# Two-block network on one Trainium2 core: the mixer's v projection as seven products of half matrices per 1024 columns, instead of eight

## The reference, cut to what matters

```python
def gmlp_mixer(h, w_in, ln_g, ln_b, w_s, b_s, w_out):
    u, v, z = jnp.split(h @ w_in, 3, axis=-1)      # h: 512 x 1024, w_in: 1024 x 6144
    u = jax.nn.gelu(u)
    v = layer_norm(jax.nn.gelu(v), ln_g, ln_b)     # v: 512 x 2048
    ...                                            # s: v mixed over tokens by w_s, plus b_s
    y = u * s * jax.nn.silu(z)
    return y @ w_out
```

## Time and profile before

| | us |
|---|---|
| median of 3 runs | 947.67 (946.54 to 948.96) |
| profiled execution, whole time | 946.47 |
| its span (first to last instruction) | 944.7 |
| PE busy | 899.6 (95%) |
| POOL busy | 637.6 (67%) |
| DVE busy | 445.0 (47%) |
| ACT busy | 282.3 (30%) |
| mean granted TensorE clock | 0.988 |
| bytes moved | 84.31 MB, mean 89 GB/s |

### The profile page before, as it was taken

How to read it: one execution, slowest core, us unless ns; L and a number is a source line. 1 busy time by engine, 2 the same in 40 slices (tenths; PEclk the granted TensorE clock), 3 DMA queues, 4 the chain that set the end, 5 groups by cost and what they waited for, 6 DMA issues and landing times.

```text
span 944.7 us, 11929 instructions
## 1 busy us (share of the span) xinstructions
PE 899.6 (95%) x4304; PEld 747.8 (79%) x4304; DVE 445.0 (47%) x782; ACT 282.3 (30%) x711; POOL 637.6 (67%) x702
## 2 busy tenths in 40 slices
PE   4999899899999989999999999999997999988997
PEld 3788788788887768888888888888876988877886
DVE  4125446755226252000844400444468868778634
ACT  4124333331225232114111111111113435765632
POOL 7677474547789667776977766777787598546343
PEclk9999999999999999999999999999999999999999
DMA  7433222233422223332222232222231222112202
GB/s 208 133 112 98 81 67 67 68 108 116 134 89 68 90 89 112 91 110 91 89 91 90 89 110 89 89 90 90 89 106 50 68 91 87 48 46 67 67 2 89
DMA packets 71866, 84.31 MB, mean 89 GB/s; under 512 B 11264, under 2 KB 53760, under 8 KB 71808
## 3 DMA queue, kind: packets, MB, share of 16 engines
q1 hardware_dynamic: 71808, 83.54, 28.1%
HBM read 81.44 MB, written 2.10 MB: 88 GB/s over the span
## 4 chain that ended last, share of the span: by engine, by line
PE 79%; DVE 8%; POOL 5%; ACT 3%; issue 2%; DMA 1%; SPq 0%; POOLq 0%; DVEq 0%; ACTq 0%
PE bank L1469 24%; PE bank L1470 24%; PE bank L1471 24%; POOL wlo L591 2%; PE bank L1636 2%; POOL ms L543 1%; POOL rstd L546 1%; ACT junk L654 1%; PE bank L1609 1%; POOL whi L584 1%; DMA resid<-in_x 1%; PE bank L1664 1%; DVE smB L1367 1%; DVE pT L1421 1%; DVE raw L1318 1%
## 5 line engine op out<-in xcount | busy, mean ns | idle before, releaser
L591 POOL TENSOR_TENSOR wlo<-raw,whi 128x512 fp32r<-128x512 f32 x280 | 383.3, 1390 | 0.0
L584 POOL TENSOR_SCALAR whi<-raw 128x512 fp32r<-128x512 f32 x280 | 184.3, 676 | 265.2 <-PE bank L1471 257.0
L1469 PE MATMUL bank<-actB_hi,whi 128*128 128x512 f32 (+1 forms) x416 | 160.0, 385 | 0.8 <-POOL wlo L591 0.8
L1470 PE MATMUL bank<-actB_lo,whi 128*128 128x512 f32 (+1 forms) x416 | 159.3, 383 | 0.0
L1471 PE MATMUL bank<-actB_hi,wlo 128*128 128x512 f32 (+1 forms) x416 | 159.2, 383 | 0.0
L1469 PE MATMUL bank<-whi,actA_hi 128*128 128x512 f32 x304 | 122.6, 403 | 7.2 <-DVE actA_lo L983 4.5
L1471 PE MATMUL bank<-whi,actA_lo 128*128 128x512 f32 x304 | 120.6, 397 | 0.0
L1470 PE MATMUL bank<-wlo,actA_hi 128*128 128x512 f32 x304 | 120.4, 396 | 0.0
L1469 PEld LDWEIGHTS bank<-actB_hi,whi 128*128 128x128 f32 x416 | 78.7, 189 | 15.5 <-DVE big L1281 0.9
L1471 PEld LDWEIGHTS bank<-actB_hi,wlo 128*128 128x128 f32 x416 | 78.6, 189 | 15.4
L1470 PEld LDWEIGHTS bank<-actB_lo,whi 128*128 128x128 f32 x416 | 78.6, 189 | 14.2
(11 more groups left out here) (205 smaller groups left out, 1340.3 us busy)
## 6 DMA issues: line engine op xcount, KB each, us to landing
raw<-in_a_w_in SPq DMA_DIRECT2D x48, 512.0 KB, 3.7
raw<-in_w_in SPq DMA_DIRECT2D x32, 512.0 KB, 3.7
raw<-in_a_w_out SPq DMA_DIRECT2D x16, 512.0 KB, 3.3
raw<-in_b_w_in SPq DMA_DIRECT2D x16, 512.0 KB, 3.4
raw<-in_w_out SPq DMA_DIRECT2D x8, 512.0 KB, 3.9
raw<-in_w_ple_gate SPq DMA_DIRECT2D x8, 512.0 KB, 3.3
raw<-in_b_w_out SPq DMA_DIRECT2D x8, 512.0 KB, 3.4
resid<-in_x SPq DMA_DIRECT2D x4, 512.0 KB, 7.9
```

Source lines behind the costliest of these rows:

```text
L584: pool.tensor_scalar(H, src[:, i * HALF:(i + 1) * HALF], 1.0, 1.0, ALU.mult, ALU.mult).then_inc(w_hi, 1)
L591: ins = pool.tensor_tensor(L, src[:, i * HALF:(i + 1) * HALF], H.bitcast(f32), ALU.subtract)
L1469: M(out_, whi_, xhi_, start=start, stop=False)
L1470: M(out_, whi_, xlo_, start=False, stop=False)
```

## The change

**The computation.** The 512 tokens by 1024 rows of h are cut into quarters: A11 is tokens 0 to 255 by the lower 512 of k, A12 the same tokens by the upper 512, A21 and A22 the other 256 tokens. A group of 1024 columns of the weights is cut into B11, B12, B21, B22 in the same way. Instead of eight products of quarters there are seven (numbered m), for each of the two groups g:

| m | activations | weights |
|---|---|---|
| 0 | A11 | B11 |
| 1 | A12 | B21 |
| 2 | A21 - A22 | B11 + B12 |
| 3 | A11 - A21 | B12 + B22 |
| 4 | A21 - A22 - A11 | B11 + B12 + B22 |
| 5 | A12 + A21 - A22 - A11 | B22 |
| 6 | A22 | B11 + B12 + B22 + B21 |

A product q = 7 g + m is two blocks `("S", "v4", q, r)` of 12 products on PE, one for each 128 of its 256 tokens. 14 products make 28 blocks, 336 products of 512 columns where there were 384. A unit now serves 24 of them, and there are 14.

**Sums of weights.** They are made in the places of the raw weights by accumulating transfers: the quarters come in the order of `LOADS7` into three places A, B (the four rows of `raw`) and G (rows 1 and 2 of `gain`), each as two halves of 512 KB; loads 3, 4, 6 and 7 of a group are issued by POOL with `accum_op=ALU.add`, on top of what lies there. SP issues the plain ones. Both wait on `w7_lo`, the count of halves that DVE has split.

**Splitting.** For these units hi is a copy of 128 x 1024 by ACT (`hi_v4`), two per unit, and lo a subtraction of 128 x 1024 by DVE (`lo_v4`), two per unit. POOL splits none of them. ACT begins a unit when PE has done the one two before.

**Sums of activations.** ACT copies each turned tile of h twice (once more in float32 into `big`); four times DVE adds quarters (`act_sum`), ACT copies (`sum_hi`) and DVE subtracts (`act_sum_lo`), all of 128 x 1024, into `actA_hi` and `actA_lo`.

**Sums of results.** Product 0 of a group is copied to `big` by ACT (`keep_v4`), and the others are added or subtracted by DVE from PSUM and `big` (`combine`, 14 of 128 x 512 per group). The gelu then works in place in `big` (`gelu_v4`).

The loads of rows 1 and 2 of `gain` for later stages move behind the last of the products. Some semaphores are merged into one, which changes no order. The scratch for descriptors of POOL's transfers is raised.

```diff
-    u += [("v4", 2 * c + kh, "T", "a_w_in_2", 4 * kh, AW + 512 * c) for c in range(4) for kh in range(2)]
+    u += [("v4", q, "S", "a_w_in_2", 0, AW + 1024 * (q // 7)) for q in range(14)]
...
+BANK7 = (4, 6, 0, 2, 4, 6, 2)
+ROOMS = {("v4", 0): "BAG", ("v4", 1): "GAB"}
+ROOM = {"A": (0, 1), "B": (2, 3), "G": (4, 5)}
+LOADS7 = (("11", 0), ("21", 1), ("12", 2), ("22", 2), ("12", 0), ("22", 1), ("22", 0), ("21", 0))
+ADDED7 = {3: (6, 7), 4: (8, 9), 6: (8, 9), 7: (8, 9)}
+OPERAND7 = (0, 1, 4, 3, 6, 5, 7)
...
-    o += [("Th", "gate", 1, 1, 3)] + turn("h", 0) + [("T", "gate", 1, 1, 3)] + turn("h", 1) + [("T", "v4", 0, 0, 0)]
-    o += turn("h", 2) + [("T", "v4", 0, 0, 1)] + turn("h", 3) + [("T", "v4", 0, 0, t) for t in (2, 3)]
-    o += [("T", "v4", 0, 1, t) for t in range(T)]
-    o += [("T", "v4", c, kh, t) for c in range(1, 4) for kh in range(2) for t in range(T)]
+    o += [("Th", "gate", 1, 1, 3)] + turn("h", 0) + [("T", "gate", 1, 1, 3), ("S", "v4", 0, 0)] + turn("h", 1)
+    o += [("S", "v4", 0, 1)] + turn("h", 2) + [("S", "v4", 1, 0)] + turn("h", 3) + [("S", "v4", 1, 1)]
+    o += [("S", "v4", q, r) for q in range(2, 14) for r in range(2)]
...
+                for h in range(2):
+                    sp.wait_ge(w7_lo, 2 * 6 + h + 1)
+                    load7("v4", 1, 2, h)
...
+            def add_load(g, nth):
+
+                q = {4: 0, 6: 2, 7: 4}.get(nth)
+                for h in range(2):
+                    dst, src, landed = quarter7("v4", g, nth, h)
+                    if q is None:
+                        pool.wait_ge(quarter7("v4", g, 2, h)[2], LANDED["v4", g, 2, h])
+                    else:
+                        pool.wait_ge(w7_lo, 14 * g + 2 * q + h + 1)
+                    pool.dma_start(dst, src, accum_op=ALU.add).then_inc(landed, 16)
+
+            after[at("gate", 3, 1)] = [lambda: add_load(0, 3), lambda: add_load(0, 4)]
+            after[at("gate", 3, 1)] += [lambda t=t: root("x2", t, D) for t in range(T)]
+            after[at("gate", 3, 1)] += [lambda g=g, n=n: add_load(g, n) for g in range(2) for n in (3, 4, 6, 7)[2 - 2 * g:]]
...
+            def hi_v4(q):
+
+                g, m = divmod(q, 7)
+                act.wait_ge(pe_block, last_block(SLOT_BEFORE[UNIT_NO["v4", q]]))
+                for h in range(2):
+                    src, H, _ = of_product("v4", q, h)
+                    act.wait_ge(quarter7("v4", g, OPERAND7[m], h)[2], LANDED["v4", g, OPERAND7[m], h])
+                    A(H, src, ACT.Copy).then_inc(w7_hi, 1)
...
+            for q in range(1, 14):
+                g, m = divmod(q, 7)
+                if m == 5:
+                    combine(g, 4, (2, 0), (2, 0), ALU.add, 0)
+                    combine(g, 2, (0, 1), (2, 0), ALU.subtract, 3)
+                    combine(g, 3, (2, 0), (2, 0), ALU.add, 3)
+                if 1 <= q <= 4:
+                    act_sum(q - 1)
+                if q < 13:
+                    lo_v4(q + 1)
+                if 1 <= q <= 4:
+                    act_sum_lo(q - 1)
+                if m == 0:
+                    combine(0, 6, (2, 0), (2, 0), ALU.add, 7)
+                if m == 2:
+                    combine(g, 1, (0, 0), (2, 0), ALU.add, 0)
+                if m == 6:
+                    combine(g, 2, (2, 1), (2, 0), ALU.subtract, 7)
+                    combine(g, 5, (0, 1), (0, 1), ALU.add, 5)
```

More of the change, by code:

```diff
@@ L2 @@
 from contextlib import ExitStack
+from itertools import count
 import concourse.bass as bass
@@ L182, in bank_of @@
             return BANKS_F[c][t]
-        return t + 4 * (1 if s == "v" else (c + (s == "v4")) % 2)
+        return t + 4 * (1 if s == "v" else c % 2)
+    if kind == "S":
+        s, q, r = b[1:]
+        return r + BANK7[q % 7]
     if kind == "s4":
@@ L634, in _ @@
             for n in range(2 * len(UNITS)):
+                if n // 2 not in WHOLE:
+                    continue
                 split_half(n)
@@ L1199, in rest_h, with lo_v4, act_sum, act_sum_lo @@
                     rest("h", t, j)
+            def lo_v4(q):
+                for h in range(2):
+                    src, H, L = of_product("v4", q, h)
+                    dve.wait_ge(w7_hi, 2 * q + h + 1)
+                    V.tensor_tensor(L, src, H.bitcast(f32), ALU.subtract).then_inc(w7_lo, 1)
+            def act_sum(i):
+                upper, lower = slice(0, S // 2), slice(S // 2, S)
+                a11, a12, a21, a22 = hT(0)[:, :, upper], hT(1)[:, :, upper], hT(0)[:, :, lower], hT(1)[:, :, lower]
+                if i == 0:
+                    dve.wait_ge(hi["h"], 2 * T)
+                else:
+                    dve.wait_ge(s7_lo, i)
+                place, first, second, op = ((a22, a21, a22, ALU.subtract), (a21, a11, a21, ALU.subtract),
+                                            (a22, a22, a11, ALU.subtract), (a22, a12, a22, ALU.add))[i]
+                V.tensor_tensor(place, first, second, op).then_inc(s7_made, 1)
+            def act_sum_lo(i):
+                dve.wait_ge(s7_hi, i + 1)
+                V.tensor_tensor(s7(actA_lo, i), hT(1 - (i == 1))[:, :, S // 2:S], s7(actA_hi, i).bitcast(f32),
+                                ALU.subtract).then_inc(s7_lo, 1)
+            def combine(g, m, place, other, op, waits):
+                for r in range(2):
+                    t, c = place
+                    u, d = other
+                    dve.wait_ge(pe_block, BLOCK["S", "v4", 7 * g + m, r])
+                    if waits:
+                        dve.wait_ge(c7_made, 14 * g + waits + r)
+                    else:
+                        dve.wait_ge(x7_kept, 2 * g + r + 1)
+                    V.tensor_tensor(out_v4(t + r, 2 * g + c), psum[bank_of(("S", "v4", 7 * g + m, r))][:, :],
+                                    out_v4(u + r, 2 * g + d), op).then_inc(c7_made, 1)
+            lo_v4(0)
             gate_in(1, 0)
             gate_in(1, 1)
-            dve.wait_ge(apre_in, 16)
+            dve.wait_ge(gain_in[0], 32)
             normed("h", "x2", 0, 0, "h")
@@ L1210, in _ @@
             normed("h", "x2", 2, 0, "h")
+            lo_v4(1)
             rest_h(2)
@@ L1505, in token_major, with seven @@
                                 kh == 0 and k == 0, kh == 1 and k == 3)
+                return ins
+            def seven(s, q, r):
+                m, n = q % 7, UNIT_NO[s, q]
+                bank = psum[bank_of(("S", s, q, r))][:, :]
+                for k in range(4):
+                    if m in (2, 3, 4, 5):
+                        aH, aL = (s7(act, m - 2)[:, k, r * P:(r + 1) * P] for act in (actA_hi, actA_lo))
+                    else:
+                        rows = slice((r + 2 * (m == 6)) * P, (r + 2 * (m == 6) + 1) * P)
+                        aH, aL = (act[:, k + 4 * (m > 0), rows] for act in (actB_hi, actB_lo))
+                    w = slice(k * HALF, (k + 1) * HALF)
+                    pe.wait_ge(w7_lo, 2 * q + k // 2 + 1)
+                    ins = exact(bank, aH, aL, whi[:, SLOT[n], w], wlo[:, SLOT[n], w], k == 0, k == 3)
                 return ins
```

241 lines of the change are left out of this document (180 added, 61 removed).

## The result

The changed kernel takes 954.67 us (median of 8 runs, 951.40 to 955.97), against 947.90 us of the kernel before on the same chip (8 runs): a ratio of 1.0061, 95% interval 1.0044 to 1.0079, so 6 to 7 us slower. The forecast was 953.0, slower. The profiled execution took 954.98 us, 8.5 more than the profiled one of before, where the sum had +5.2. So the direction held and the sum was 3.3 us too small in that execution.

What follows compares the result with a forecast made beforehand. PE, busy 95% of the span, was taken as the bound. -1.1 with weights in time and +6.3 for late additions made +5.2: 951.7 against the profiled 946.47, with 1.2 for the median 953.0 us, range 944 to 962.

Steps and rivals of the forecast that it cites:

- the sum: Whole change: -1.1 us with the weights in time, +6.3 for late accumulating transfers, together +5.2 us.
- What TensorE loses, -10.9 us: PE in v4: 384 products become 336, 48 x 0.227 us less, all on the path.
- The start of v4: First blocks on tiles 0, 1 and 3 wait for their operands: PE idles 1.0, 1.75 and 1.3 us.
- Product 2: In v4: operands ready at 367.6 after a row of DVE steps; PE idles 4.8 us before it.
- The clock behind an idle stretch, 1.7 us: PE at a granted clock of 0.50: 1.7 us added to each idle stretch of 2 us or more.
- The accumulating transfers, 3.4 us per half: Weight sums in v4: an accumulating half costs two plain transfers of 1.7 us; issue on POOL 1.0 us.
- Product 9: In v4: load 4 of the second group late, start 412.1 instead of 407.5; idle 4.6 and 1.7 of clock, +6.3.
- z4: Its start: POOL's split of the first unit takes 7.38 us against 5.44; idle 2.3 and 1.7 us of clock.
- (a): Rival: the additions are hidden, a half costs under 2.2 us: -1.1, 946.6 us; chance 0.26.
- (b): Rival: additions hidden, idle stretches under the clock's limit, DVE's chain before product 2 1 us shorter: 944 us; chance 0.12.
- (c): Rival: an addition costs three passes, 5.1 us per half: some +15, 962 us; chance 0.20 with cases between.
- (d): Rival: the change does not do what it says; the order shows 336 products, so nothing was left to it.

Runs made afterwards that it cites:

- e1_plain: The changed kernel with GpSimd's 32 transfers overwriting their destination instead of adding to it: 948.53 us, ratio 0.9998 to the kernel before.
- e2_swap: The changed kernel with GpSimd issuing load 4 of group 2 ahead of its load 3: 949.98 us, ratio 1.0014 to the kernel before.
- e5_p2: The changed kernel with the second product's operands made earlier by reordering ScalarE's and VectorE's steps: 951.11 us, ratio 1.0041 to the kernel before.
- the repetition: The changed kernel again, unaltered, timed on another chip: 954.24 us, ratio 1.0075 to the kernel before.
- e4_z4half: The changed kernel with z4's first block started on the first half of its weights: 952.41 us, ratio 1.0049 to the kernel before.
- e3_late5: The changed kernel with SyncE's load 5 of group 2 held back by one product more: 951.31 us, ratio 1.0039 to the kernel before.
- e6_filler: The changed kernel with 22 discarded matmuls while TensorE waits for product 2's operands: 951.43 us, ratio 1.0047 to the kernel before.
- e7_all: The changed kernel with the edits of e2_swap, e4_z4half and e5_p2 together: 944.38 us, ratio 0.9965 to the kernel before.

## Why the prediction came out as it did

- **What TensorE loses, -10.9 us.** Right: x4256 for x4304 at the old pace of 0.227 us, and e1_plain and e2_swap show products 3 to 13 nearly without a wait.
- **The start of v4.** Right within half a microsecond at each step: the blocks of tiles 0 and 1 were forecast at 346.45 and 351.75 and started at 346.76 and 352.15, tile 3's transposes at 359.73 for 359.3. The new steps were priced well: DVE's 1024 columns took 1.22 us, ScalarE's 1.06.
- **Product 2.** Forecast 367.6, measured 367.83. That DVE's row of steps sets it held, and e5_p2 showed it by changing their order.
- **The clock behind an idle stretch, 1.7 us.** This term was too small. From 367.83 to 373.08 twelve products took 5.25 us where 2.72 is full pace: +2.5, and over the whole product 2.6. I had taken the price from one stretch of ten products; here the low clock lasted longer. At product 9 it was worse: the clock was low until some 421. That the second wait of 0.54 us drew it out is a guess. In the repetition, with one wait, product 9 took 2.1 us more than full pace, against 4.7 here; but in e4_z4half, with a second wait of 0.98 us, it was 2.7, that wait included.
- **The accumulating transfers, 3.4 us per half.** 3.12 measured, so the choice of two plain ones (1.60 each) held. By the Trainium skill, "Collectives: The Full Stack", section "The bandwidth ceiling: the fold count and why AG ≠ RS ≠ AR", the reduce step of a ring collective runs at half the rate of a copy, since an addition has two source reads. This transfer is no collective, but its factor of 1.95 agrees. The issue took 1.2 us for my 1.0.
- **Product 9.** Forecast 412.1, measured 412.10, but by luck. I let the second half decide, landing at 411.0; in fact the first, at 409.6, set the start, and the second, at 413.2, made TensorE wait again. TensorE also came 1.0 us later than forecast, at 408.5 for 407.5, so its wait was shorter. In the repetition the start is 53.9 us behind the transposes, not 52.4. The step that failed is the one that counted only GpSimd's own four halves in the queue: a plain load of SyncE's moved beside them, and e3_late5 showed that by holding it back. From 412.1 on, the remaining five products took 444.03 - 412.10 = 31.9 us, where the sum had 5 x 5.44 + 1.7 = 28.9: **+3.0 us**, 0.9 of it the second wait, the rest the clock. This is nearly all of the 3.3 us by which the sum fell short. The repetition splits it otherwise, a later start and then 29.3 us; from the transposes to the end of product 13 the two profiles are 2.6 and 1.5 us above the forecast's 81.7.
- **z4.** Idle 2.85 us from start to start for 2.3 forecast: +0.55. GpSimd's second subtraction took 2.93 us for the 2.54 that I had read the earlier trace rows, and its slot came free when product 12 ended, as forecast. The clock behind it cost 1.6 us for 1.7 in this execution, and nothing in the repetition.
- **The sum.** +5.2 became +8.5 in the profile and 6.8 in the medians. Of the rivals, (a), hidden additions, is what e1_plain and e2_swap make: 948.5 and 950.0, not 946.6; 1.0 us of that is the dearer clock behind product 2, 0.5 the wait at `z4`, and the rest is not accounted for. In (b) I had doubted that the clock must fall behind `z4`'s wait, and rightly, see below; but it asked for hidden additions and a shorter product 2 as well. (c) is out by the measured price. (d) is out by the count.

## What to carry to other kernels

When a change removes work from the engine that bounds the kernel, walk through every operand that it will now ask for earlier, and price each late one as the wait plus the half clock behind it (for one wait of 2 to 5 us, between nothing and 2.8 us here). Look at the order of a queue before its cost: here one swap of two transfers gave back most of the loss, and nothing was made cheaper. Count what other queues move at the same time, because the engines are shared. In these runs a gain upstream was kept where the transfers are released by the work itself (e5_p2), and mostly lost where the next step is a chain on another engine (e4_z4half).

## What the runs showed of the hardware

- An accumulating transfer from HBM into SBUF, 512 KB, took 3.12 us of the 16 DMA engines for 1.60 of the plain one from the same queue, and landed 6.1 to 14.3 us after its issue (median 8.0; plain 4.2 to 7.5). GpSimd spent 1.22 to 1.27 us to issue one, and 0.72 without the addition; SyncE's plain ones took 0.37.
- The same idle stretch does not always lower the clock. Ahead of `z4` TensorE waited 2.70 us in the changed kernel, in its repetition and in e2_swap; behind it the granted clock fell to 0.57 in the first (window above) and stayed at 1.00 in the other two (in the repetition up to 456). The windows of TensorE at that place in the repetition and in e2_swap:

```profile
446.00:448.00 2.00, 2.00 (x10) 1.00 0.63 186
```

```profile
440.00:450.00 10.00, 9.34 (x41) 7.77 (x42) 1.50 (x5) 8.55 (x9) 9.58 (x14) 1.00 0.43 130
```

  Behind the same wait it fell in e1_plain and e5_p2 too, and stayed in e3_late5 and e6_filler. Behind the 4.28 us at product 2 it fell every time. What decides it I haven't tested. It is one reason why two executions of a kernel differ by a microsecond or two.
- 22 matmuls whose result nobody reads made the kernel faster: idle TensorE is not free, since it is slower afterwards. Whether such filling also pays on top of e7_all, where the wait is 2.0 us, was not tried.
